# A two-layer streaming trunk in float32: the norm factor moved behind the products, the output projection and the MLP joined in one block

## The reference

```python
def rmsnorm(x, g):
    y = x * rsqrt(mean(x * x, axis=-1) + EPS)
    return y * g

# layer A (l = 0)
hn = rmsnorm(h, norm_attn[0]);  q, k, v = split(hn @ w_qkv_a)      # q, k rotated
o = rmsnorm(diff_attend(q, k, v), subln_a) * (1 - 0.2)            # per head of 128
h = h + o @ w_o_a
h = h + square(relu(rmsnorm(h, norm_mlp[0]) @ w_up[0])) @ w_down[0]
# shared K/V and layer B (l = 1)
kvf = rmsnorm(h, norm_kv) @ w_kvf                                  # K, V and 16 forget columns
q = rmsnorm(h, norm_attn[1]) @ w_q_b
h = h + fox_attend(q, kvf) @ w_o_b
h = h + square(relu(rmsnorm(h, norm_mlp[1]) @ w_up[1])) @ w_down[1]
y = rmsnorm(h, norm_final)
```

## Time and profile before

| What | Value |
|---|---|
| Median of 3 runs | 3873.42 us |
| Span of the profiled execution (the page gives no time beside it) | 3875.0 us |
| TensorE matmul busy | 3483.5 us, 90% |
| TensorE weight load busy | 2992.9 us, 77% |
| VectorE busy | 1676.6 us, 43% |
| ScalarE busy | 1099.1 us, 28% |
| GpSimd busy | 478.8 us, 12% |
| Mean granted TensorE clock | 0.955 |
| DMA | 345.93 MB, mean 89 GB/s |

### The profile page before, as it was taken

How to read it: one execution, slowest core, us unless ns; L and a number is a source line. 1 busy time by engine, 2 the same in 40 slices (tenths; PEclk the granted TensorE clock), 3 DMA queues, 4 the chain that set the end, 5 groups by cost and what they waited for, 6 DMA issues and landing times. The chain is left out here.

```text
span 3875.0 us, 59511 instructions
## 1 busy us (share of the span) xinstructions
PE 3483.5 (90%) x22994; PEld 2992.9 (77%) x22994; DVE 1676.6 (43%) x2828; ACT 1099.1 (28%) x2118; POOL 478.8 (12%) x188
## 2 busy tenths in 40 slices
PE   6998887886799999999799978877978799999998
PEld 5886776765699999999588767765656799999997
DVE  4432886545444444444212156643432344444445
ACT  3001664433211111222202046642332221121112
POOL 2110000002011111111211000000001111111110
PEclk9998998998899999999799989988998899999999
DMA  4223443972111111110212143427762111111111
GB/s 141 90 81 85 93 92 112 337 289 89 60 38 38 43 43 43 43 43 11 72 61 90 52 95 77 84 61 231 276 229 71 49 43 43 43 43 43 43 43 49
DMA packets 284887, 345.93 MB, mean 89 GB/s; under 512 B 155136, under 2 KB 204448, under 8 KB 284768
## 3 DMA queue, kind: packets, MB, share of 16 engines
q1 hardware_dynamic: 262352, 296.18, 24.7%
q10 hardware_dynamic: 20128, 39.93, 2.9%
q0 software_dynamic: 2304, 8.39, 0.7%
HBM read 300.46 MB, written 43.98 MB: 89 GB/s over the span
## 5 line engine op out<-in xcount | busy, mean ns | idle before, releaser
L772 DVE TENSOR_TENSOR h_rows<-h_rows,m_dn 128x512 f32<-128x512 f32 x576 | 391.4, 686 | 325.4 <-PE m_dn L346 325.4
L344 PE MATMUL m_dn<-m_dn_hi,m_hid_hi 128*128 128x512 f32 x1152 | 449.4, 390 | 0.0
L345 PE MATMUL m_dn<-m_dn_lo,m_hid_hi 128*128 128x512 f32 x1152 | 448.4, 389 | 0.0
L346 PE MATMUL m_dn<-m_dn_hi,m_hid_lo 128*128 128x512 f32 x1152 | 448.2, 389 | 0.0
L756 DVE TENSOR_TENSOR m_relu<-m_relu 128x384 f32<-128x384 f32 x192 | 157.3, 819 | 515.2 <-ACT m_relu L737 515.2
L344 PE MATMUL m_up<-b_xt_hi,m_up_hi 128*128 128x384 f32 x768 | 261.7, 341 | 17.1 <-POOL m_up_lo L677 17.1
L344 PE MATMUL m_up<-c_xt_hi,m_up_hi 128*128 128x384 f32 x768 | 262.0, 341 | 15.1 <-POOL m_up_lo L677 15.1
L677 POOL TENSOR_TENSOR m_up_lo<-m_up_raw,m_up_hi 128x2048 fp32r<-128x2048 f32 x32 | 147.6, 4614 | 931.4 <-ACT m_up_hi L727 931.4
L346 PE MATMUL m_up<-c_xt_hi,m_up_lo 128*128 128x384 f32 x768 | 259.6, 338 | 0.0
L345 PE MATMUL m_up<-c_xt_lo,m_up_hi 128*128 128x384 f32 x768 | 259.6, 338 | 0.0
L345 PE MATMUL m_up<-b_xt_lo,m_up_hi 128*128 128x384 f32 x768 | 259.4, 338 | 0.0
(11 more groups left out here) (328 smaller groups left out, 6943.2 us busy)
## 6 DMA issues: line engine op xcount, KB each, us to landing
da_k_tiles<-in_cache_a_k SPq DMA_DIRECT2D x64, 512.0 KB, 5.8
da_v_tiles<-in_cache_a_v SPq DMA_DIRECT2D x64, 512.0 KB, 5.2
m_up_raw<-in_w_up SPq DMA_DIRECT2D x32, 1024.0 KB, 5.3
m_dn_raw<-in_w_down SPq DMA_DIRECT2D x32, 1024.0 KB, 4.8
db_k_tiles<-in_cache_b_k SPq DMA_DIRECT2D x64, 512.0 KB, 4.9
db_v_tiles<-in_cache_b_v SPq DMA_DIRECT2D x64, 512.0 KB, 4.9
qkv_w_raw<-in_w_qkv_a SPq DMA_DIRECT2D x24, 512.0 KB, 4.0
pa_k_dup<-out_ak_p SPq DMA_DIRECT2D x32, 256.0 KB, 4.4
```

The source lines that it names most:

```text
L344: pe.matmul(out, lh, rh, start=start, stop=False)
L345: pe.matmul(out, lh, rl, start=False, stop=False)
L346: return pe.matmul(out, ll, rh, start=False, stop=stop)
L772: dve.tensor_tensor(hc, hc, dns[n % 3][:], ALU.add).then_inc(s_de, 1)
```

## The change

- A row is turned with its gain but without its factor (`gained`), and the factor, one column per row tile (`row_factor`, `rstd`), is put on the product where it is taken out of PSUM. In the MLP its square goes on the down products (`m_factor`, `r2`). The squares of h for it are summed by ScalarE beside the turns.
- Rows for kv are turned with neither gain nor factor, straight from `h_rows`. The gain goes on the weights: VectorE scales each raw part (`scale`) before ScalarE makes its high part. So the query of layer B uses the same turned rows as K and V, and the second turn of all rows in kv is gone. The forget products move from the first piece to the second.
- The head norm puts only its factor on the rows. Its gain and 0.8 go on the parts of `w_o_a` (`weight_scale`).
- `start_phase` is gone. Its constants are loaded in the qkv block, lambda is worked out at the end of that block.
- `post_phase` is output projection and MLP in one block: piece 0 over all rows, then piece 1 over all rows with the turns for the MLP two rows behind it, then the 16 steps. The first up weights are loaded and split during the passes.
- `clear_semaphores` is called in three more places: behind da, pb and db.

```diff
-def start_phase(nc, core, table, lams):
...
-class Norm:
...
-        if self.own_rows:
-            dve.scalar_tensor_tensor(x, self.core.h[:, r, :], self.rstd[:, r, 0:1], self.gain[:], ALU.mult,
-                                     ALU.mult).then_inc(self.s_xn, 1)
-        else:
-            own(dve.tensor_tensor(xh, xh, self.rstd[:, r, :].unsqueeze(2).to_broadcast([P, 8, P]), ALU.mult))
-            dve.tensor_tensor(xh, xh, self.gain[:].unsqueeze(1).to_broadcast([P, 8, P]),
-                              ALU.mult).then_inc(self.s_xn, 1)
...
-def mlp_phase(nc, core, tag, w_up, w_down, following, y_rows=None):
...
-                for n in range(ND):
-                    r, c = n // 2, n % 2
-                    hc = core.h[:, r, c * HALF:(c + 1) * HALF]
-                    dve.wait_ge(s_dm, i * ND + n + 2)
-                    dve.tensor_tensor(hc, hc, dns[n % 3][:], ALU.add).then_inc(s_de, 1)
-                    if last and c and r:
-                        nxt.vector(dve, r - 1)
...
+def project_phase(nc, core, tag, pieces, gains, first=None, forget=None):
...
+            if first:
+                sp.dma_start(core.h[:, 0, :], rows_of(*core.x, 0)).then_inc(s_row[0], 16)
+                sp.dma_start(core.const[:], table).then_inc(s_c, 16)
+                load(0)
+                load(1)
+                for r in range(1, 3):
+                    sp.dma_start(core.h[:, r, :], rows_of(*core.x, r)).then_inc(s_row[r], 16)
...
+            def gained(r):
+                if r == 0:
+                    dve.wait_ge(s_g, 16)
+                if r >= 2:
+                    dve.wait_ge(s_tp, 2 * r - 2)
+                dve.wait_ge(s_row[r], 16)
+                dve.tensor_tensor(xn[:, r % 2, :], core.h[:, r, :], gain[:], ALU.mult).then_inc(s_xn, 1)
...
+            def scale(n):
+                i, k = n // PARTS, n % PARTS * KP
+                dve.wait_ge(s_raw[n % 2], 16 * (n // 2 + 1))
+                for j in range(KP):
+                    ins = dve.tensor_scalar(raw[:, n % 2, j, :], raw[:, n % 2, j, :],
+                                            gcol[:, pieces[i][4], k + j:k + j + 1], None, ALU.mult)
+                ins.then_inc(s_sc, 1)
...
+                if do == "store":
+                    dve.tensor_scalar(o, src_, rstd[:, r:r + 1], None, ALU.mult).then_inc(s_ev, 1)
+                    return
...
+def post_phase(nc, core, tag, ao, w_o, head_gain, w_up, w_down, gain_mlp, last=None):
...
+            load_row(0)
+            load_w(0)
+            load_w(1)
+            load_row(1)
+            for n in range(2, PARTS):
+                load_w(n)
+            sp.dma_start(gain[:], gain_mlp.partition_broadcast(P)).then_inc(s_gm, 16)
+            for r in range(2, RT):
+                load_row(r)
+                if r + 2 < 2 * PARTS:
+                    load_w(r + 2)
+            sp.wait_ge(s_olo, 2 * PARTS)
+            with sp.Fori(0, STEPS) as i:
+                sp.wait_ge(s_ul, i + 1)
+                sp.dma_start(up_raw[:], w_up[:, bass.ts(i, FC)].rearrange("(k p) n -> p k n", p=P)).then_inc(s_ur, 16)
...
+            turn_o(0)
+            for r in range(RT):
+                if r + 1 < RT:
+                    turn_o(r + 1)
+                pe.wait_ge(s_lo, 2 * r + 2)
+                out_unit(0, r)
+            for r in range(RT):
+                out_unit(1, r)
+                if r >= 2:
+                    turn_h(r - 2)
+            def step(i, begin=False, end=False):
+                pe.wait_ge(s_ul, i + 2)
+                for g in range(RG):
+                    if begin:
+                        pe.wait_ge(s_lo, 2 * RT + 2 * (g + 1) * (RT // RG))
+                    for f in range(NF):
+                        n = g * NF + f
+                        pe.wait_ge(s_hl, i * NU + n + 1)
+                        if begin and n < 3:
+                            pe.wait_ge(s_oe, 2 * RT)
...
+                        ins.then_inc(s_um, 1)
+                        if begin and n < 2:
+                            turn_h(RT - 2 + n)
...
+                    if end and not last and r >= 1:
+                        turn_last(r - 1)
+            def turn_last(r):
+                pe.wait_ge(s_de, (STEPS - 1) * ND + 2 * r + 2 + 3)
+                turn(2 * RT + r, h[:, r, :])
...
+            for r in range(RT):
+                square(r)
+                if r == 1:
+                    act.wait_ge(s_om, RT)
+                    up_high(0)
+                high(RT + r)
...
+                    dve.scalar_tensor_tensor(hc, dns[n % 3], r2[:, r:r + 1], hc, ALU.mult,
+                                             ALU.add).then_inc(s_de, 1)
+                    if end and c and r >= 1:
+                        last_factor(r - 1)
+                        if not last and r >= 2:
+                            low(2 * RT + r - 2)
+                        elif last:
+                            last_scale(r - 1)
...
+            if head_gain is not None:
+                head_norm(0)
+                weight_scale(0)
+                weight_scale(1)
+                head_scale(0)
+            for r in range(RT):
+                if head_gain is not None and r + 1 < RT:
+                    head_norm(r + 1)
+                    if r == 0:
+                        weight_scale(2)
+                        weight_scale(3)
+                    if 2 <= r < 6:
+                        weight_scale(r + 2)
+                    head_scale(r + 1)
+                low(r)
+                if r:
+                    out_add(0, r - 1)
+            out_add(0, RT - 1)
+            for r in range(RT):
+                out_add(1, r)
+                gained(r)
+                if r:
+                    low(RT + r - 1)
+                factor(r)
+            low(2 * RT - 1)
...
-        start_phase(nc, core, a["const"],
-                    [a[n] for n in ("lambda_q1", "lambda_k1", "lambda_q2", "lambda_k2")])
...
-            dense_phase(nc, core, "oa", "head", a["subln_a"][0, :], ao,
-                        [(a["w_o_a"].rearrange("n d e -> (n d) e"), c, "add", c) for c in (0, HALF)],
-                        following=a["norm_mlp"][0, :])
-            mlp_phase(nc, core, "m0", a["w_up"][0], a["w_down"][0], a["norm_kv"])
-            core.clear_semaphores()
...
+            project_phase(nc, core, "qkv",
+                          [(wa, c, "rope", (*qd, c), 0) for c in (0, HALF)]
+                          + [(wa, D + c, "rope", (kv["ak_p"], kv["ak_s"], c), 0) for c in (0, HALF)]
+                          + [(wa, 2 * D + c, "store", (kv["av_p"], kv["av_s"], c), 0) for c in (0, HALF)],
+                          gains, first=(a["norm_attn"][0, :], a["const"], lams))
...
+        core.clear_semaphores()
+            post_phase(nc, core, "m0", ao, a["w_o_a"].rearrange("n d e -> (n d) e"), a["subln_a"][0, :],
+                       a["w_up"][0], a["w_down"][0], a["norm_mlp"][0, :])
+            core.clear_semaphores()
+            project_phase(nc, core, "kv",
+                          [(wkv, c, "store", (kv["bk_p"], kv["bk_s"], c), 0) for c in (0, HALF)]
+                          + [(wkv, D + c, "store", (kv["bv_p"], kv["bv_s"], c), 0) for c in (0, HALF)]
+                          + [(wq, c, "store", (*qd, c), 1) for c in (0, HALF)],
+                          gains,
+                          forget=(wkv[:, 2 * D:2 * D + 16], a["b_f"], fp, fs))
...
```

807 lines of the change are left out of this document (443 added, 364 removed).

## The result

The kernel after takes 3773.26 us, the median of 4 runs (3766.13 to 3775.46); the kernel before, timed beside it, 3875.33. The ratio is 0.9728, 95% interval 0.9698 to 0.9758. The profiled execution of after has a span of 3773.3 us and a time of 3774.97, against a span of 3875.0 for before. So there are 101.7 us to account for in the two traces.

The account below looks back on a forecast made before the run. TensorE's own work was taken as the bound, MLP steps full and time open at block borders. Terms -14.7 - 24.0 + 2.7 - 10.6 + 1.4 - 20.9 = -66.1 us gave 3807 us from the median 3873.42; range 3788 to 3834.

Parts of the forecast that it names:

- parts 1, 2, 4 and 6: Start and qkv, layer A projection into MLP, kv, layer B projection into MLP: -14.7, -24.0, -10.6, -20.9 us.
- places 1 to 6: Start and qkv -14.7, layer A projection -24.0, m0's last step +2.7, kv -10.6, db border +1.4, layer B projection -20.9 us.
- the chain of parts ahead of the first product: At the start, four weight parts through two buffers take 13 to 14 us; first product at 24.6 us.
- the add that releases the first unit up: Behind the output projection, the first unit up waits for VectorE's last add, 4.3 us.
- the square held by GpSimd: First MLP step: GpSimd's low part of the down weights holds the first square of relu up to 4.6 us.
- part 1: Start and qkv: first product -11.0 us, first nine units -4, lambda's end +0.3; sum -14.7 us.
- part 2: Layer A output projection into MLP: start -5.7, passes -5.9, behind them -12.4; sum -24.0 us.
- part 6: Layer B output projection into MLP: start +1.0, passes -11.2, behind them -10.7; sum -20.9 us.
- part 3: Last step of m0: rows of 5.9 us with waits of 1.9, 51.7 us where 49 was measured: +2.7 us.
- Rival 1: Clock drops in m0's last step (9 us) and weight parts at the starts come late (8 us): 3824 us, 18%.
- Rival 2: MLP scaled adds held by GpSimd: 3871 us, no change (4%), or slower, 3919 if the clock drops too (5%).
- Rival 3: Merged block doesn't start its MLP earlier, so the 12.4 and 10.7 us are gone: 3830 us, 3%.

Follow-up runs that it names:

- The two padded kernels: Unused bytes only: before padded to operand distances of multiples of 256 bytes, 3847.0 us; after padded by 128 bytes, 3806.09 us.
- start_weights_first: Kernel after with first weight loads ahead of row 0 and the constants, and ScalarE's first two high parts ahead of everything else: 3770.04 us, ratio 0.972.
- up_weights_late: Kernel after with ScalarE taking the high part of the first up weights only behind the output projection's last product, load still early: 3786.86 us, ratio 0.9768.

## Why the prediction was wrong

**The step that failed** stands in its first part: "The change leaves the matmuls of a step as they are, so these 1546 us of both layers stay", and with it the price of 5.60 us for each of 144 units in parts 1, 2, 4 and 6. The matmuls stayed as they are, their operands did not stay where they are. Priced by what each unit took in the two traces: 54 units of qkv by 0.16 is 8.6, 54 of kv by 0.135 is 7.3, 36 of the output projections by 0.12 to 0.14 is 5, and 32 steps by 0.26 is 8.3: 29 us of the 35.6 that were missing. The two padded kernels show about the same sum in time, 27.6 and 33 us (31 of the latter where the padding acts). A working on before's rows could have seen it coming only as a bound: the two speeds of six equal matmuls (1.40 and 1.36 us) stood in the trace, the forecast noted "5.60 / 4 = 1.4 us or a little less" and didn't ask why. That the addresses moved the time down and not up is chance: nothing in the change was meant to place them.

**What held.** Without the new unit, the places 1 to 6 come to -11.7 (forecast -14.7), -25 (-24.0), +0.3 (+2.7), -12.0 (-10.6), +0.8 (+1.4) and -23 (-20.9), which with attention A is -73 in place of -66: the other 7 us of the miss are small terms. The steps by which they were worked out are the ones in the trace: the chain of parts ahead of the first product, the add that releases the first unit up, the square held by GpSimd (4.61 for "up to 4.6"), rows of the last step bound by a low part behind two adds, the forget products that now cost their time in every row.

**Terms mis-sized.** In part 1 the first product was put at 24.6 and came at 27.07: -8.6 instead of -11.0. The order of ScalarE, row 0 ahead of the first part, and the longer low parts of GpSimd were left out; start_weights_first shows that this order, with that of the loads, costs 5.0 us there. In part 2 what lies behind the passes gained 13.5 (12.4) and in part 6 13.4 (10.7): the forecast charged a slow restart to the new kernel, and the old first steps had one too (51.22 and 51.88 us for 49.77). The passes of part 6 gained 12.2 (11.2), some 2.5 of it the new unit. In part 3 the last step took 50.0 us, not 51.7, with rows of 5.71 for 5.9, and the border with cleared semaphores 0.93, not 1.65.

**Rivals.** Rival 1: the clock stayed at 1.00 through the last step with waits of 1.78 us in each row, so none of the six rows paid, and the starts were held in part only. Rival 2: no hold, 0.75 us beside GpSimd. Rival 3: the up weights were there in time; up_weights_late shows that late parts would have cost 7.8 and 9.0 us, less than the 12.4 and 10.7 taken.

The 2.1 us of attention A need no cause: in the profiles with that attention's code and addresses as in the kernel before it took 511.6 to 514.5 us, and with those of the kernel after 508.6 to 517.0. Open is why a distance costs what it does between two operands, and why 16 bytes on the moving one cost too.

## What to carry to other kernels

When tensors are added, dropped or put in another order, the addresses behind them move, and with them the time of matmuls that nobody touched; so before a unit's time is carried over, look whether equal shapes have two speeds in the trace, and compare the operands' addresses. For float32 products of 512 columns keep the stationary and the moving operand a multiple of 256 bytes apart, and the moving one at a multiple of 32 (shown by three units only); a few unused bytes do it. And a wait for another engine can go by order alone: a turn one row later, weight parts rows or loads earlier. Three such orders gave 28 us here.
